# Three edits to the order of work where an MLP round changes from its up to its down products

## The reference

```
h = rmsnorm(x, norm2_g)
x = x + square(relu(h @ w_ff1)) @ w_ff2      # w_ff1: 1024 x 4096, w_ff2: 4096 x 1024
return rmsnorm(x, final_g)
```

## Time and profile before

| | |
|---|---|
| median of three runs | 1430.40 us |
| the profiled execution's own time | 1430.91 us |
| its span, first to last instruction | 1429.2 us |
| TensorE busy | 1403.6 us, 98% |
| VectorE busy | 998.8 us, 70% |
| ScalarE busy | 716.4 us, 50% |
| granted TensorE clock, mean | 0.997 of full speed |

### The profile page before, as it was taken

One profiled execution on the slowest core, in us unless ns is written; L12 is line 12 of the kernel. 1 busy time (PEld: TensorE's weight loads), 2 busy tenths in 40 slices (PEclk: granted clock), 3 DMA queues, 4 the chain that ended last, 5 costly groups with the idle time before them and its releaser, 6 DMA issues.

```text
span 1429.2 us, 18878 instructions
## 1 busy us (share of the span) xinstructions
PE 1403.6 (98%) x6653; PEld 1154.0 (81%) x6653; DVE 998.8 (70%) x1973; ACT 716.4 (50%) x1383; POOL 160.0 (11%) x176
## 2 busy tenths in 40 slices
PE   9999999999999999999999999999999999999997
PEld 7778787888878888788888778787878888787886
DVE  6253447878787888866558977868596868777654
ACT  6111236666665666722225654645464555555464
POOL 2000000010101010000140021120203030202100
PEclk9999999999999999999999999999999999999999
DMA  6364351221221222365222156473819183745553
GB/s 209 106 200 121 104 148 45 60 63 55 61 67 41 64 59 64 126 230 163 93 91 96 56 103 130 78 136 78 159 53 164 50 161 76 135 101 112 110 162 118
DMA packets 159804, 151.73 MB, mean 106 GB/s; under 512 B 12276, under 2 KB 124712, under 8 KB 159713
## 3 DMA queue, kind: packets, MB, share of 16 engines
q1 hardware_dynamic: 143584, 121.20, 27.8%
q0 software_dynamic: 16128, 29.37, 14.0%
HBM read 94.43 MB, written 56.10 MB: 105 GB/s over the span
## 4 chain that ended last, share of the span: by engine, by line
PE 89%; DVE 7%; ACT 2%; issue 2%; SPq 0%; DMA 0%; DVEq 0%; POOL 0%; ACTq 0%; POOLq 0%
PE psU L1917 7%; PE psU L1919 7%; PE psU L1918 7%; PE psU L2342 4%; PE psU L2306 4%; PE psU L2305 4%; PE psU L2307 4%; PE psX L2135 4%; PE psU L2344 4%; PE psU L2343 4%; PE psX L1917 3%; PE psX L1918 3%; PE psX L1919 3%; PE psX L2305 3%; PE psX L2306 3%; PE psX L2307 3%
## 5 line engine op out<-in xcount | busy, mean ns | idle before, releaser
L878 POOL DMA_DIRECT2D residual_scratch<-csum x112 | 98.3, 911 | 493.5 <-DVE csum L1820 424.2
L1643 DVE TENSOR_TENSOR ring_lo<-raw,ring_hi 128x512 fp32r<-128x512 f32 x150 | 103.2, 688 | 71.8 <-ACT ring_hi L1130 71.8
L1917 PE MATMUL psU<-ahi,whi 128*128 128x512 f32 x352 | 139.3, 396 | 0.2 <-DVE alo L1329 0.2
L1919 PE MATMUL psU<-ahi,wlo 128*128 128x512 f32 x352 | 137.5, 391 | 0.0
L1918 PE MATMUL psU<-alo,whi 128*128 128x512 f32 x352 | 137.5, 391 | 0.0
L1021 ACT ACTIVATE pth<-psX 128x512 fp32r<-128x512 f32 x148 | 88.2, 596 | 85.7 <-PE psX L2135 85.5
L1130 ACT ACTIVATE ring_hi<-raw 128x512 fp32r<-128x512 f32 x150 | 92.6, 624 | 63.7 <-PE psU L2344 23.3
L1546 DVE TENSOR_TENSOR ptl<-psX,pth 128x512 fp32r<-128x512 f32 x132 | 90.8, 688 | 32.6 <-ACT pth L1021 31.7
L1917 PE MATMUL psX<-ahi,whi 128*128 128x512 f32 x256 | 108.5, 424 | 1.7 <-ACT zst L1035 1.5
L1013 ACT ACTIVATE prob<-prob,nb 128x640 f32<-128x640 f32 (+7 forms) x128 | 93.4, 731 | 24.2 <-DVE nb L1522 24.1
L1918 PE MATMUL psX<-alo,whi 128*128 128x512 f32 x256 | 100.7, 393 | 0.0
(11 more groups left out here) (331 smaller groups left out, 3729.8 us busy)
## 6 DMA issues: line engine op xcount, KB each, us to landing
raw<-in_w_ff_dram SPq DMA_DIRECT2D x120, 256.0 KB, 4.4
residual_scratch<-csum POOLq DMA_DIRECT2D x112, 256.0 KB, 5.8
wraw<-in_w_in_dram SPq DMA_DIRECT2D x31, 512.0 KB, 4.1
gate_scratch<-zst SPq DMA_DIRECT2D x32, 256.0 KB, 3.5
mg<-gate_scratch SPq DMA_DIRECT2D x16, 512.0 KB, 3.4
proj_scratch<-stage SPq DMA_DIRECT2D x15, 512.0 KB, 3.0
xt<-in_x_dram SPq DMA_DIRECT2D x8, 512.0 KB, 7.0
qraw<-proj_scratch SPq DMA_DIRECT2D x32, 128.0 KB, 2.9
```

Of the source, the lines that this page charges most:

```text
L878: pool.dma_start(resid[rows, cols], sums[b][e][:], accum_op=ALU.add).then_inc(added[b][e], 16)
L1643: nc.vector.tensor_tensor(lo, raw_of(g), hi.bitcast(f32), ALU.subtract).then_inc(w_lo, 1)
L1917: nc.tensor.matmul(ps, whi[:, slot, w], hi[:, k, cols], start=start, stop=False)
L1919: return nc.tensor.matmul(ps, wlo[:, slot, w], hi[:, k, cols], start=False, stop=stop)
```

## The change

Three things are moved, at the round change of each round but the last (7 times in an execution):

- ScalarE: the square of pair 2r+1's fourth block (`hidden_hi(p, 3)`) is issued ahead of item_hi(17), where it was behind it. The copy of item 14's half 0 is issued ahead of the high parts of S2 and S1. The copy of half 1 stays between S1 high and S3 high.
- VectorE: combine(16) (the raw block for the weights of item 18) is issued after S1 low, where it was after item_lo(16), ahead of the relu.
- VectorE: the sum S3, which the text of the change calls the fourth sum, is issued ahead of the low part of S1, where it was behind it.

No instruction is added or taken away, and every wait stays as it is.

```
--- before.py
+++ after.py
                         if tail and k == RP:
+                            copy_down(r, d, i, 0)
                             hidden_sums_hi(p - 1, ("S2", "S1"))
-                        if k >= RP and i in COPY_AT:
+                            copy_down(r, d, i, 1)
+                            hidden_sums_hi(p - 1, ("S3", "S4"))
+                        elif k >= RP and i in COPY_AT:
                             for e in range(2):
                                 copy_down(r, d, i, e)
-                        if tail and k == RP:
-                            hidden_sums_hi(p - 1, ("S3", "S4"))
+                        last = k == RP - 1 and i == I_T4 and r < ROUNDS - 1
+                        if last:
+                            hidden_hi(p, HID_AT[i])
                         item_hi(g + RING)
...
-                        if k < RP and i in HID_AT and p + HID_AT[i]:
+                        if k < RP and i in HID_AT and p + HID_AT[i] and not last:
                             hidden_hi(p, HID_AT[i])
...
                             hidden_sums(p - 1, ("S1", "S2", "S4"))
-                            hidden_sums_lo(p - 1, ("S2", "S1"))
+                            hidden_sums_lo(p - 1, ("S2",))
                             hidden_sums(p - 1, ("S3",))
+                            hidden_sums_lo(p - 1, ("S1",))
+                            combine(g - 2 + RING)
                         if tail:
                             item_lo(g - 1 + RING)
                             combine(g - 1 + RING)
...
                             item_lo(g + RING)
-                            combine(g + RING)
+                            if k != RP - 1 or i != I_B22 or r == ROUNDS - 1:
+                                combine(g + RING)
```

## The result

The changed kernel takes 1422.67 us (median of five runs, 1421.33 to 1424.59) where the one before takes 1430.42: a ratio of 0.9949, 95% interval 0.9937 to 0.9960, so half a percent faster. The forecast was 1422.8 us, 7.6 us less. From the first down product (item 14 of the first round) to the end the profiles have 1429.2 - 827.04 = 602.16 us before and 1421.4 - 826.84 = 594.56 after: 7.60 us less. The other 0.2 us of the difference in span lies ahead of item 14's first start, where the kernels are the same.

A forecast was written before the change was run, and what follows sets the result against it. TensorE, busy 98% of the span, was taken as the bound, losing 1.08 us at each round change. Winning 6 x 1.08 + 1.14 = 7.6 us gave a forecast of 1422.8 us, range 1421.2 to 1427.0.

The forecast's parts named there:

- What bounds it: Whole kernel: TensorE, busy 98% of the span, loses 1.08 us at each round change, more than the 0.59 us idle shown.
- The releaser of item 16's half 0: At item 16's start: TensorE waits for ScalarE's copy of item 14's half 0; the late start costs 0.83 us.
- The square and combine(16) need each other: Front of both queues: without combine(16) moved, the square could not start before 906.99; together S1 gains 0.54 us.
- the margin of 0.09 us before half 1: Item 16's half 1: with S3 earlier, its copy releases TensorE at 911.25, against a no-loss limit of 911.34.
- Item_lo(17) has 0.33 us to spare: At item 17: item_lo(17) releases TensorE at 912.37, limit 912.70, leaving 0.33 us where it had 1.4.
- The first round change: VectorE is 0.35 us later there; loss 1.40 us, half 1 still 0.26 us too late, so 1.14 us won.
- The loads: Weight blocks for the next set: 0 and 2 issued no sooner, 1 and 3 1.1 us earlier; cost nothing.
- The sum: All seven round changes: 6 x 1.08 + 1.14 = 7.6 us won, between bounds of 0 and 7.9 us.
- case A: Round changes: half 1's copy keeps its 0.25 us loss; 6.1 us won, 1424.3 us, at worst 1426.5; chance 0.12.
- case C: Same round: later loads or weights hold TensorE again by 1.08 us; no change, 1430.4 us; chance 0.06.
- Case B: VectorE's queue: four neighbours step 0.73 us, not 0.60, delaying half 1 and item 17; 6.2 us won, 1424.2; chance 0.04.
- D: ScalarE's queue: half 0's copy or item_hi(17) holds it, making item 17 late; held 2.5 us, 1434.6 us; chance 0.03.

The follow-up runs named there:

- all but the copy: Changed kernel with the copy of item 14's half 0 put back behind S2 and S1 high: 1423.55 us, 0.9964 of the kernel before.
- the change again: The changed kernel itself, unaltered, measured once more: 1422.47 us, 0.9945 of the kernel before.
- the first four experiments: In text order: only half 0's copy moved, 1430.11 us; only S3 moved, 1429.00; both, 1426.89; changed kernel with that copy put back, 1423.55.
- all but the square: Changed kernel with the square put back behind item_hi(17) on ScalarE: 1423.99 us, 0.9960 of the kernel before.

## Why the prediction was right, point by point

- *What bounds it.* TensorE, with one loss of 1.08 us in each round, found from the starts and not from the 0.59 us of idle time. Right: the round fell by 77.26 - 76.18 = 1.08 us. Two small misses cancel in that number: the loss was 1.10 (77.26 less the 76.16 of the version with S3 ahead of S2 low), and 0.02 of it is left.
- *The releaser of item 16's half 0*, which the profile gave as "issue", is the first copy. Right: with the copy alone moved, item 16 starts on pace and nothing else has changed ahead of it.
- *The square and combine(16) need each other.* Right in the main: without the square 0.36 us of a round's gain goes, without combine(16) 0.45. Beside copy and S3, the square without combine(16) is worth nothing that shows (76.63 against 76.67), as forecast; combine(16) without the square is worth 0.1, where the prediction had nothing. Neither was run alone.
- *S3, and the margin of 0.09 us before half 1.* Right, and the finest number of the sum. Later by 0.60 and 1.20 us, S3 cost 0.52 and 1.13 us a round. The release so near to the limit does cost 0.02 to 0.04 us, which the version with S3 still earlier has back. The prediction took its limit from 912.51, while its own rows give 912.53 (913.89 less 6 x 0.2267): a limit of 0.13 us ahead of the on-pace start and not 0.11, and so margins of 0.07 here and 0.31 at item 17. Against the pace of 76.16 the experiments give 0.06 and 0.29.
- *Item_lo(17) has 0.33 us to spare.* Right within 0.04: 0.60 later, it costs 0.28 to 0.29.
- *The first round change.* 0.26 us late was forecast, 0.30 measured; the loss before was 1.43 (836.63 less 827.04, less 8.16) and not 1.40, so what is won, 1.13 to 1.15, is the 1.14 forecast.
- *The loads* cost nothing: matmuls wait nowhere from 829 to 1413 us. VectorE does wait for a raw block in the rounds, which the prediction did not mention, before as after the change, in the first round longer than before; none of it reaches TensorE:

```profile
DVE t L1656 <- DMA raw<-in_w_ff_dram: 6.9, 7, 1.4
...
DVE t L1660 <- DMA raw<-in_w_ff_dram: 8.1, 7, 2.7
```

- *The sum*: 7.6 us forecast, 7.60 measured from item 14 on. That the median too came within 0.2 us of the forecast is partly luck, since single times lie on levels some 1.5 us apart (last section).
- *Two slips without effect.* 23 steps in 5.21 us are 0.2265 each, not 0.2267; the pace of 0.2267 is that of the whole round (76.16 / 336). And ScalarE's step was taken as 0.60 from a pair in which the second waited; without a wait it is 0.52 to 0.54.

One step was wrong, though the result did not hang on it: the price of case A, "If it keeps its old loss of 0.25 us, 7 x 0.83 + 0.32 = 6.1 us are won". That splits the loss into 0.83 and 0.25 us as if they were paid one after the other. But the second copy waits for S3 and not for TensorE. When only the first wait goes, TensorE runs into the second one at its old time, and 0.03 us of 1.08 is won, not 0.83. The sum of case A holds only if half 1 comes 0.25 us behind the pace for a reason of its own; that only the first part goes means no change in time, as the run with the copy alone shows, and belonged with case C. The range did not cover that.

Case B fell. The four neighbours S3, S1 low, combine(16), item_lo(17) start 0.60 us apart each (908.49, 909.09, 909.69, 910.29), before the 0.68 us of the one ahead has run out. For case B I had cited the Trainium skill, "VectorE: DVE Perf Modes", section "The DRAIN you can't avoid". That section also says that an operation which is not held starts earlier, and refers to the section "Two Vector instructions with no wait between them"; I left that exception out. The rows agree with the exception. They do not agree that a wait costs nothing, where it is for the instruction just ahead: 0.73 us from S1 to S2, which needs it, against 0.60. Cases C and D did not occur; the one margin that C named, 0.33 us at item 17, is real.

## What to carry to other kernels

When an engine waits twice in a row for things that other engines make, the two idle times are not two prices: compute for each wait when its release comes, on the clock of the engine that makes it, and take the latest against the on-pace start. Edits to such a chain can be worth little one by one (here 0.03 and 0.23 us a round) and much together (0.59, and 1.08 with the rest), so an edit that shows no gain alone is not yet refused. Read the loss from the starts of the work against its pace, since waits hidden behind overlapped instructions show no idle time.

## What the runs showed that I had not expected

- **Where the spread of single times lies.** The first item 14 starts at 825.05, 825.08, 825.14, 826.25, 826.51, 826.79, 826.84 (twice), 827.04, 827.66, 828.24, 828.27 and 828.50 us in the thirteen profiles, though no kernel differs in what TensorE does ahead of it. From there a round repeats within 0.05 us. What differs most is TensorE's granted clock: from 105 to 120 us its mean is 1.00 in the first three profiles, 0.89 in the next seven and 0.77 in the last three, with 84, 77 and 70 matmuls. Three such rows (columns as in the earlier trace rows), of "all but the copy", the change and the change again, and last a piece of that stretch in the change again:

```profile
105.00:120.00 15.00, 15.00 (x84) 12.99 (x83) 8.94 (x10) 1.82 (x3) 0.00 (x0) 1.00 0.54 140
105.00:120.00 15.00, 15.00 (x77) 12.92 (x76) 8.61 (x10) 1.81 (x3) 0.00 (x0) 0.89 0.54 143
105.00:120.00 15.00, 15.00 (x70) 12.82 (x69) 8.40 (x10) 1.13 (x2) 0.00 (x0) 0.77 0.53 140
111.50:114.20 2.70, 2.70 (x8) 2.22 (x9) 2.02 (x3) 1.13 (x2) 0.00 (x0) 0.50 1.06 241
```

  So there is a short stretch at the lower of the two levels, 1.2 GHz and not 2.4, which is absent, short or twice as long, and 7 matmuls of 0.227 us are 1.6 us. Within the seven profiles the start still varies by 1.4 us, for which no cause was found. The recorded times show the same steps: the 27 runs of the kernel before that were made beside the first four experiments lie at 1428.59 to 1428.92, 1429.81 to 1430.65 and 1431.81 to 1433.06 us, and none between. A median of five can fall on one step or another: in "all but the copy" and "all but the square" three of five runs are on the lowest, which fits medians that are lower than their rounds would have them. Just ahead of the stretch TensorE runs the same 32 matmuls of two columns (L2028) in these three profiles, whether the clock falls or not; what decides it stays open.
- **The price of starting late.** When TensorE starts a matmul late, the one behind it comes 0.31 to 0.34 us later instead of 0.227, at every late start seen (911.15 less 910.84 before the change, 914.01 less 913.67 with combine(17) first). So a wait that ends too late costs about 0.1 us on top of its length. This is the same thing as the limit of the prediction: a release has to come about 0.1 us ahead of the on-pace start to cost nothing.
